# Residual sums as products on TensorE, turned tiles on four banks, and one weight item split by GpSimd in a two-block transformer

## The reference

```python
for i in range(DEPTH):                                     # first block
    h, gate = adaln_norm(x, c, norm_g[i], ada_w[i], ada_b[i])
    y = nsa_mixer(h, ...) if i % 2 == 0 else dilated_mixer(h, dil_w_in, dil_w_out)
    x = x + gate * y
x = rms_norm(x, final_g)
for layer in range(DEPTH):                                 # second block
    mix = _mixer_ab(x, ...) if layer % 2 == 0 else _mixer_cd(x, ...)
    x = _layer_norm(DEEPNORM_ALPHA * x + mix, ln1_g[layer], ln1_b[layer])
    ffn = (silu(x @ w_gate) * (x @ w_up)) @ w_down         # width 2816
    x = _layer_norm(DEEPNORM_ALPHA * x + ffn, ln2_g[layer], ln2_b[layer])
```

## Time and profile before

| what | value |
|---|---|
| median of 3 runs | 1098.12 us (1096.86 to 1101.09) |
| the profiled execution's own time | 1096.86 us |
| its span, first to last instruction | 1095.1 us |
| mean granted TensorE clock | 0.974 |
| busy TensorE, VectorE, ScalarE, GpSimd | 92%, 59%, 43%, 10% |

### The profile page before, as it was taken

How to read it: one execution, slowest core, us unless ns; L and a number is a source line. 1 busy time by engine, 2 the same in 40 slices (tenths; PEclk the granted TensorE clock), 3 DMA queues, 4 the chain that set the end, 5 groups by cost and what they waited for, 6 DMA issues and landing times.

```text
span 1095.1 us, 15848 instructions
## 1 busy us (share of the span) xinstructions
PE 1005.4 (92%) x6078; PEld 849.6 (78%) x6078; DVE 648.6 (59%) x1118; ACT 475.8 (43%) x740; POOL 114.3 (10%) x106
## 2 busy tenths in 40 slices
PE   5989989889998998898999999997998889999994
PEld 2889655668997778877778888876997768888884
DVE  4346354774662566535766666666454586666666
ACT  1243543624455623475334444433447534444440
POOL 3004101310970001100010000000001000000000
PEclk9999998999999899998999999999999999999997
DMA  9953254334452445321464554532532154555440
GB/s 378 354 203 131 88 221 154 119 152 150 157 210 83 187 148 185 120 77 40 166 219 172 184 206 184 178 145 93 213 141 78 70 187 166 180 206 189 172 172 39
DMA packets 23382, 178.41 MB, mean 163 GB/s; under 512 B 3711, under 2 KB 4143, under 8 KB 6823
## 3 DMA queue, kind: packets, MB, share of 16 engines
q1 hardware_dynamic: 19120, 166.70, 41.3%
q0 software_dynamic: 2224, 8.94, 2.4%
q10 hardware_dynamic: 1991, 2.14, 0.6%
HBM read 176.72 MB, written 1.05 MB: 162 GB/s over the span
## 4 chain that ended last, share of the span: by engine, by line
PE 75%; DVE 15%; ACT 4%; DMA 3%; issue 2%; ACTq 1%; POOL 0%; SPq 0%; DVEq 0%; POOLq 0%
PE G L858 12%; PE G L860 12%; PE G L859 12%; PE S L953 8%; PE T L953 7%; PE S L952 3%; PE T L952 3%; PE T L523 3%; PE T L442 2%; PE G L537 1%; PE G L539 1%; PE G L538 1%; DVE wlo L1624 1%; PE G L381 1%; DVE wlo L1621 1%
## 5 line engine op out<-in xcount | busy, mean ns | idle before, releaser
L858 PE MATMUL G<-whi,hTh 128*128 128x256 f32 (+4 forms) x688 | 222.5, 323 | 14.0 <-DVE hTl L459 5.5
L859 PE MATMUL G<-wlo,hTh 128*128 128x256 f32 (+4 forms) x672 | 211.1, 314 | 0.0
L1722 DVE TENSOR_TENSOR wlo<-ring,whi 128x2048 fp32r<-128x2048 f32 x88 | 154.4, 1758 | 90.3 <-ACT whi L1409 64.8
L860 PE MATMUL G<-whi,hTl 128*128 128x256 f32 (+4 forms) x624 | 192.3, 308 | 0.0
L858 PEld LDWEIGHTS G<-whi,hTh 128*128 128x128 f32 x688 | 132.4, 192 | 22.8 <-DVE hTl L459 7.1
L1621 DVE TENSOR_TENSOR wlo<-ring,whi 128x1024 fp32r<-128x1024 f32 (+2 forms) x60 | 92.7, 1586 | 68.5 <-ACT whi L1307 68.3
L859 PEld LDWEIGHTS G<-wlo,hTh 128*128 128x128 f32 x672 | 129.5, 193 | 3.7 <-issue 1.3
L953 PE MATMUL S<-hT,whi 128*128 128x512 f32 x352 | 129.3, 401 | 3.3 <-DVE hT L459 3.3
L953 PE MATMUL T<-hT,whi 128*128 128x512 f32 x352 | 126.5, 394 | 0.0
L860 PEld LDWEIGHTS G<-whi,hTl 128*128 128x128 f32 x624 | 120.5, 193 | 0.7
L1404 ACT CAST whi<-ring 128x2048 fp32r<-128x2048 f32 x44 | 83.9, 1906 | 17.9 <-PE S L1019 17.6
(11 more groups left out here) (305 smaller groups left out, 1823.8 us busy)
## 6 DMA issues: line engine op xcount, KB each, us to landing
ring<-in_ffn SPq DMA_DIRECT2D x44, 1536.0 KB, 6.3
ring<-in_ada_w SPq DMA_DIRECT2D x16, 1024.0 KB, 5.3
ring<-in_dil_w_in SPq DMA_DIRECT2D x16, 1024.0 KB, 4.8
ring<-in_cd_w_in SPq DMA_DIRECT2D x10, 1232.0 KB, 5.3
ring<-in_nsa_w_in SPq DMA_DIRECT2D x8, 1432.0 KB, 8.8
early<-in_ada_w SPq DMA_DIRECT2D x8, 1024.0 KB, 17.2
ring<-in_ab_w_in SPq DMA_DIRECT2D x4, 1440.0 KB, 6.2
vec<-in_vecs POOLq DMA_DIRECT2D x11, 512.0 KB, 5.0
```

The lines of the kernel that those rows point to most:

```text
L858: pe.matmul(out_, act_h, w_h, start=first_, stop=False)
L859: pe.matmul(out_, act_h, w_l, start=False, stop=False)
L860: return pe.matmul(out_, act_l, w_h, start=False, stop=last_)
L1722: TT(wlo[b][:, part], ring[:, b, part], whi[b][:, part].bitcast(F32), ALU.subtract).then_inc(st[what + "_lo"], 1)
```

## The change

- **Residual as a product.** In the second block's FFNs, TensorE multiplies ALPHA times the identity (`alpha_ident`, in `tok`) by `x` into the FFN's output banks ahead of its products (`residual`), which then accumulate on top. `ffn_out` reads the banks directly for statistics and for the subtraction.
- **Halves.** The last step of each LayerNorm is written in two halves of 512 columns, each with its own signal; turns and the store of the output go by halves.
- **Border order.** `dn`'s first low part comes after the turn's low parts; in `cd_in` both items of the first chunks are split before tile 1's norm, and the second chunk is whole before tile 1's turn; uq's low part comes after the latents' turns.
- **Entrances.** The `_rot` turns use four banks; ScalarE copies even groups and VectorE odd ones. Groups of later heads (four each in dil, ab and cd) are turned inside pairs 0 and 1, in G2 and G3, and copied by VectorE.
- **GpSimd.** It makes high and low parts of item 1 of `ab_out` and `cd_out`, once the entrance's turns are out.
- **Sinks.** No accumulation on ScalarE's exponentials; the sinks are exponentiated by themselves and added to the sums that the product with v already gives.
- **dil.** The gate is multiplied in per pair, the shares later, for tile 0 on VectorE and for tile 1 on ScalarE; the low parts of dil_out's items move (`low_quarters` makes item 0's in quarters, two at p = 8 and two behind the shares).

```diff
+        APART = ("ab_out", "cd_out")
...
+        alpha_ident = tok[:, 0, 0:P]
+        def bank_of(name, j, t):
+            return G[2 * t + j] if name == "cd_in" else G[2 * j + t]
...
+            if name in APART and m == 1:
+                return item_low, APART.index(name) + 1
...
+        SHARED = ("nsa_rot", "dil_rot", "ab_rot", "cd_rot")
...
+        SHARED_BANKS = TB + S
+        def wait_turned(eng, name):
+            groups, _, t0, _, _ = turns[name]
+            eng.wait_ge(turn["taken"], t0 + (len(groups) + 1) // 2)
+            eng.wait_ge(turn["drawn"], drawn0[name] + len(groups) // 2)
...
-                if g >= 2 and turn_bank(name, g) is turn_bank(name, g - 2):
+                if g >= 4 and name in SHARED:
+                    pe.wait_ge(*((turn["drawn"], drawn0[name] + g // 2 - 1) if g % 2 else (turn["taken"], t0 + g // 2 - 1)))
...
+                if name in SHARED and g % 2 == 1:
+                    continue
...
+        def turn_draw(dve, name):
+            groups, g0 = turns[name][0:2]
+            for g in range(1, len(groups), 2):
+                dve.wait_ge(turn["turned"], g0 + g + 1)
+                take = groups[g][1][0]
+                dve.tensor_copy(take[2], turn_src(name, g, take)).then_inc(turn["drawn"], 1)
+        def weave_turn(pe, name, k):
+            if k >= 2:
+                pe.wait_ge(woven["taken"], woven0[name] + k - 1)
+            for b, (src, width) in enumerate(woven_groups[name][k][0]):
+                ins = pe.transpose(G[3 - k % 2][0:width, b * P:(b + 1) * P], src, ident)
+            ins.then_inc(woven["turned"], 1)
+        def weave_draw(dve, name, k):
+            dve.wait_ge(woven["turned"], woven0[name] + k + 1)
+            rows, cols, dst, n = woven_groups[name][k][1][0]
+            dve.tensor_copy(dst, G[3 - k % 2][rows[0]:rows[1], cols[0]:cols[1]].rearrange("p (n c) -> p n c", n=n)).then_inc(woven["taken"], 1)
...
+                if sink is not None and 2 * p < n and sink(2 * p) is not None:
+                    rows = slice(2 * p, 2 * p + 2)
+                    dve.wait_ge(att["maxes"], 2 * (b0 + 2 * p + 2))
...
+                        dve.wait_ge(ab_s["sink_exp"], p - 5)
+                        summed = den[:, rows, :].unsqueeze(3)
+                        done(TT(summed, summed, o[:, :, :, DH:DH + 1], ALU.add))
...
-                            act_.activation(s[:, 0:1 + P], s[:, 0:1 + P], ACT.Exp, bias=negmax[:, h, 0:1], scale=-1.0,
-                                            accum_out=den[:, h, 0:1]).then_inc(att["probs"], 1)
...
+                        act_.activation(s[:, 1:1 + P], s[:, 1:1 + P], ACT.Exp, bias=negmax[:, h, 0:1], scale=-1.0).then_inc(att["probs"], 1)
+                        act_.activation(s[:, 1 + P:1 + SW], s[:, 1 + P:1 + SW], ACT.Exp, bias=negmax[:, h, 1:2],
+                                        scale=-1.0).then_inc(att["probs"], 1)
...
+                    if sink(2 * p - 2):
+                        rows = slice(2 * p - 2, 2 * p)
+                        act_.wait_ge(ab_s["sink_in"], p - 4)
+                        act_.activation(den[:, rows, :], den[:, rows, :], ACT.Exp).then_inc(ab_s["sink_exp"], 1)
...
-        dil_rot = rows_to(qT, blocks_of(tok)) + rows_to(kT, blocks_of(rotk))
+        dil_rot = [dil_q[0], dil_q[2], dil_k[0], dil_k[2]]
...
+        woven_groups = {"dil": [dil_q[1], dil_q[3], dil_k[1], dil_k[3]],
+                        "ab": rows_to(q2T, blocks_of(u[:, :, 672:1184])) + rows_to(q2T[:, 4:6, :], blocks_of(kswa)),
+                        "cd": rows_to(q2T, blocks_of(u[:, :, 1544:2056])) + rows_to(q2T[:, 4:8, :], blocks_of(u[:, :, 2056:2568]))}
...
-                sp.wait_ge(norm["ready"], norm_ready(8) - 1 + t)
-                sp.dma_start(out[:, t * P:(t + 1) * P, :].rearrange("b p d -> p (b d)"), x[:, t, :]).then_inc(stored, 16)
+                for half, (sig, value) in enumerate(((norm["half"], norm_half(8) + 1 + t), (norm["ready"], norm_ready(8) - 1 + t))):
+                    cols = slice(half * 512, (half + 1) * 512)
+                    sp.wait_ge(sig, value)
+                    sp.dma_start(out[:, t * P:(t + 1) * P, cols].rearrange("b p d -> p (b d)"), x[:, t, cols]).then_inc(stored, 16)
...
+            def split_item(name):
+                n = first[name] + 1
+                pool.wait_ge(landed[n % 2], 16 * (n // 2 + 1))
+                pool.wait_ge(used, split0[name] - 1)
+                raw, half = ring[:, n % 2, 0:OUT_K * OUT_W], OUT_K * OUT_W // 2
+                for part in range(2):
+                    cols = slice(part * half, (part + 1) * half)
+                    tl.done(pool.tensor_copy(out_high(1)[part], raw[:, cols]))
+                    ins = pool.tensor_tensor(out_low(1)[part], raw[:, cols], out_high(1)[part].bitcast(F32), ALU.subtract)
+                ins.then_inc(item_low, 1)
...
+            wait_turned(pool, "ab_rot")
+            split_item("ab_out")
...
-                chunk_part(1, 0, range(KT // 2))
+                turn_after = KT if name == "cd_in" else KT // 2
+                ins = chunk_part(1, 0, range(turn_after))
...
                 turn_pe(pe, turn_name, ready, 1)
-                chunk_part(1, 0, range(KT // 2, KT)).then_inc(st["full"], 1)
+                if turn_after < KT:
+                    chunk_part(1, 0, range(turn_after, KT)).then_inc(st["full"], 1)
                 if behind is None:
...
+            def residual(i, t, free):
+                pe.wait_ge(ffn[i]["alpha_set"], 1)
+                pe.wait_ge(outp["taken"], free)
+                for half in range(2):
+                    pe.matmul(G[2 * t + half][:], alpha_ident, x[:, t, half * 512:(half + 1) * 512], start=True, stop=False)
...
-                down(0, 0, True, False)
+                down(0, 0, False, False)
...
+                    if name in APART and n == 1:
+                        pe.wait_ge(item_low, APART.index(name) + 1)
...
+                        pe.wait_ge(*((norm["ready"], norm_ready(i) - 1 + g // 2) if g % 2 else (norm["half"], norm_half(i) + 1 + g // 2)))
...
+            def second_half(name, i, base):
+                def behind(p):
+                    if p < 2:
+                        weave_turn(pe, name, 2 * p)
+                        weave_turn(pe, name, 2 * p + 1)
+                    if p == 2:
+                        pe.wait_ge(woven["taken"], woven0[name] + 4)
+                    if p == 8:
+                        turn_half(i, 0, att["outs"], base + 4)
+                return behind
+            att_pe(pe, "ab", second_half("ab", 2, pairs0))
             project_out(2, "ab_out", None, (att["outs"], pairs0 + 8), "f0", norm_tiles(5))
-            keep_busy(5)
+            residual(0, 0, 11)
+            keep_busy(4)
             turn_pe(pe, "f0", norm_tiles(5), 1)
...
                 high(name, 0, 0, KT * w)
+                if name == "cd_in":
+                    high(name, 0, 1, KT * w)
                 turn_act(sc_e, turn_name, 0)
-                high(name, 0, 1, KT * w)
+                if name != "cd_in":
+                    high(name, 0, 1, KT * w)
...
+            sc_e.wait_ge(dil_s["share"], 1)
+            for g in range(3):
+                cols = slice(offs[g] * DH, offs[g + 1] * DH)
+                ins = sc_e.activation(tok[:, 1, cols], tok[:, 1, cols], ACT.Copy, scale=share[:, 1, g:g + 1])
+                if g > 0:
+                    ins.then_inc(shared_ready, 1)
...
-                    if p == 2:
-                        high_out(name, 1)
...
+            def scale_halves(i, b, t):
+                for half, sig in enumerate((norm["half"], norm["ready"])):
+                    cols = slice(half * 512, (half + 1) * 512)
+                    done(STT(x[:, t, cols], x[:, t, cols], rstd[:, t:t + 1], b[:, cols], ALU.mult, ALU.add), sig)
...
+            def set_gated(p, o, summed, r):
+                set_pair(p, o, summed, r)
+                cols = slice(2 * p * DH, (2 * p + 2) * DH)
+                done(TT(tok[:, :, cols], tok[:, :, cols], u[:, :, 3 * D + 2 * p * DH:3 * D + (2 * p + 2) * DH], ALU.mult))
...
+                if gatev is None:
+                    done(TS(alpha_ident, ident, ALPHA, None, ALU.mult), ffn[i - 2]["alpha_set"])
...
                 turn_low(dve, turn_name, 1)
+                low_ffn(st, 0, 0, dn, "dn")
                 low_ffn(st, 0, 1, gu, "gu")
...
+            def ffn_out(i, name, n, g, b, turn_name=None, lows=None):
...
+                    moments([G[2 * t + half][:] for half in range(2)], t, 2, True, EPS_LN)
                     for half in range(2):
-                        part = x[:, t, half * 512:(half + 1) * 512]
-                        done(STT(part, part, ALPHA, G[2 * t + half][:], ALU.mult, ALU.add))
-                        done(dve.bn_stats(bstat[:, t, half, :], part))
-                    finish(t)
+                        cols = slice(half * 512, (half + 1) * 512)
```

(45 more changed lines are left out.)

157 lines of the change are left out of this document (99 added, 58 removed).

## The result

The changed kernel took 1070.07 us as a median of four runs (1065.55 to 1073.16), beside 1099.2 for the kernel before (also four runs); the ratio is 0.9724, with a 95% interval of 0.9679 to 0.9770. The ratio times the 1098.12 of the table is 1067.8: 30 us gained, where 22 were forecast. The profiled execution took 1067.20 us against 1096.86, 29.7 less, with a sum of 22.3 to hold against it.

What follows compares the result with a forecast made beforehand. It took TensorE, with 75% of the chain (VectorE 15%), to bound the kernel, with gains only where it stands. Terms summed to 22.3 us: 1096.86 - 22.3 = 1074.6, plus 1.26, gave 1076, range 1069 to 1086.

Steps and rivals of the forecast that it cites:

- dil out: Before dil's last turns: gating moved into eight pairs, shares split over two engines, to gain 1.0 us [0 to 1.8].
- latents: Before ab: uq's low part, moved behind the latents' first low part, removes most of TensorE's 4.03 us wait: 2.4 gained.
- below 1069 only if nearly every high end holds: Whole kernel: a time under 1069 us needs almost all terms at their high ends; all high ones give 1068.
- ab's pairs: ab attention: without item 1's splits, seven pairs follow at 3.05 us each; with sinks' 0.4, 5.0 gained [2 to 6.5].
- the idle that preceded the 0.81 is gone: First FFN's first 9 us: 1.7 us of full clock is lacking, and half, 0.9, comes back.
- wanted only by the first down product: Borders into FFNs: dn's low part, 1.14 us of VectorE, can come behind the turn's low parts.
- Woven turns: Attentions: head groups turned inside the first pairs cost TensorE 2.2 us in dil and 1.65 in ab and cd.
- GpSimd's item: ab and cd: four GpSimd instructions for item 1 take 10.3 us clean or 32.6 contended, costing 0, up to 3 lost.
- Pairs bound by TensorE at 3.4: Rival, chance 0.15: attention pairs stay at 3.4 us, the sum falls to 14.4, the time is 1084 us.
- Residual products exposed: Rival, chance 0.07: at FFN borders, 7.1 us of products less two fillers gives 5.3 back; 1081 us.
- GpSimd late: Rival, chance 0.05: TensorE waits for item 1 in both projections, 3 us in each; 1082 us.
- Slower: Rival, chance 0.02: GpSimd takes 47 us for four instructions, ending at 528 and 880; 1104 us.

Runs made afterwards that it cites:

- e1: The kernel before, run again without an edit for a second trace: 1104.39 us.
- e9: The changed kernel with cd_in's start in the old order (second item's low part behind tile 1's norm, half the second chunk behind the turn, old banks): 1068.50 us, single execution.
- e8: The changed kernel with the residual of both FFNs added by VectorE again and one full-width subtraction: 1077.91 us, single execution.
- e3: The changed kernel with dn's first low part back ahead of the turn's low parts: 1072.15 us.
- e7: The changed kernel with uq's low part ahead of the latents' low parts again: 1073.88 us, single execution.
- e4: The changed kernel with GpSimd's three bias loads put off until four low parts of dn are done in the first FFN: 1069.64 us.
- e6: The changed kernel with all turns of the four entrances on two banks, drawn by ScalarE, none woven into pairs: 1074.02 us, single execution.
- e11: The changed kernel run again without an edit for a third trace: 1074.27 us, ratio 0.9813 to the kernel before.
- e12: The kernel before, run again without an edit for a third trace: 1090.47 us.
- e2: The changed kernel, run again without an edit for a second trace: median 1074.06 us, ratio 0.9833 to the kernel before.

## Why the forecast was right in its parts and 8 us short in the first comparison

Stages of the changed kernel against those of before, each from the trace with the least clock lost in it:

| term of the sum | forecast | before | changed | gain |
|---|---|---|---|---|
| start and nsa entrance | 0.4 | 117.61 | 117.26 | 0.35 |
| dil entrance and pairs | 1.4 | 35.67 | 33.59 | 2.1 |
| dil out, to x0's turn | 1.0 | 35.19 | 32.54 | 2.7 |
| x0's turn to ab's turn (latents) | 2.4 | 61.08 | 57.15 | 3.9 |
| ab entrance and pairs | 5.0 | 38.28 | 31.36 | 6.9 |
| ab_out | 0 | 30.23 | 30.39 | -0.2 |
| border ahead of the first FFN | 0.65 | 8.59 | 7.65 | 0.94 |
| first FFN | 0.9 | 184.55 | 187.35 | -2.8 |
| first FFN's end to tile 1's turn | 4.9 | 19.80 | 14.92 | 4.9 |
| cd entrance and pairs | 1.4 | 34.54 | 31.71 | 2.8 |
| border ahead of the second FFN | 0.65 | 8.58 | 7.65 | 0.93 |
| second FFN | 0.9 | 183.16 | 183.14 | 0 |
| end | 2.7 | 13.83 | 11.31 | 2.5 |
| sum | 22.3 | | | 25.1 |

The sum of the last column agrees with all executions together: 25 of the kernel before have their median at 1097.99, 14 of the changed one at 1073.05, 24.9 apart. This backs the sum and not each row, since the rows take the traces with the least clock lost, and an execution loses more. By the means of three traces each, the changed kernel is 29.4 faster: 4.0 of that is the nsa stage, which has no row, cd's row is 4.5 (e1's falls), ab's is 5.6, and ab_out is 1.3 slower and not 0.2. The new wait of 1.9 at ab's entrance, for VectorE's draws, has a fall behind it in two of the changed kernel's three traces.

**The step that failed: "below 1069 only if nearly every high end holds".** 1067.8 came, with more than half of the high ends not reached. Between the two profiled executions 29.7 us were gained, 7.4 more than the sum. Of these 29.7, 8.4 lie ahead of the end of dil_in: 4.0 in the start, where the sum had 0.4, and 4.4 from there through the nsa attention, its projection and dil_in, where it had nothing (219.34 against 214.95, with 6.8 and 3.4 of clock lost). The change has next to nothing in that stretch, and the kernel before took 222.90 and 214.41 there in its other traces. I had made the range from bounds of costs alone and put the difference between executions of one kernel at nothing. The three comparisons gave ratios of 0.9724, 0.9833 and 0.9813; on 1098.12 the last two are 1079.8 and 1077.6, in the range. Behind dil_in the pair of traces gained 21.3 where the sum had 21.9. That this comes so close is luck: several terms were too low, by up to 2.3 (dil out), one was too high by 4.6 (the first FFN), and one of -1.8 (ab_out) I did not have.

**Right, with its size.** cd_in's start (4.9 forecast, 4.9 measured, e9), the end (2.7 and 2.5, e8), both borders (0.65 and 0.94), the dil entrance itself (2.79, forecast 2.9), ab's entrance (1.8, forecast 1.7) with the wait for VectorE's draws where I put it, and ab's pairs at 2.9 to 3.0, forecast 3.05, but for the first of 2.70 and one of 3.38. The end's 2.5 is two errors that nearly cancel: VectorE saved 0.94 a tile and not 1.4, and the last store gave 0.6 where I took next to nothing. GpSimd ran in attention at no more than its clean price (2.37 for 1024 columns, where two rows of 512 give 2.58). With that the trace agrees with the Trainium skill (GPSIMD Engine Reference, 1. Specifications), by which GpSimd contends with VectorE's instructions in a two-port mode or with two SBUF inputs; VectorE's maxima beside it read PSUM and one table.

**A step of the sum that failed: "the idle that preceded the 0.81 is gone: 9 us at 0.81 lack 1.7 us of full clock; I take half, 0.9".** I charged the clock at two borders only. At the first FFN it does come back once the new wait is away (184.55 to 183.05 in e3, 1.5 for my 0.9); the second FFN has no fall in the first two traces of before and could return nothing. Clock is lost behind other waits which this change also shortens. Behind the latents' wait it is 1.7 to 3.1 in the three traces of before and 0 in the changed kernel's; e7 puts the wait back and gets 4.7 for my 2.4. That term came out 1.5 over, and the clock is the reason. Dil out lost 5.1 in all three traces of before and 0, 5.1 and 0 in the changed kernel's. In ab's pairs the clock (3.4 in all three of before, none at the casts' place in the changed kernel's) also came back, but my step from the measured turns to a pace of 3.05 already held it without naming it; ab's 1.9 over is some 0.75 of hidden woven turns, and the rest a pace just under 3.05 and the sinks' 0.4, which did not show. The earlier trace rows showed the 0.62 there, and I used it for a rival instead of asking where else waits are followed by it.

**A second one: dn's low part, "wanted only by the first down product".** It was wanted by the ring as well. I followed item_low through the ring of two slots and not this one. Its new place lets the slot go 9.5 us later against the FFN's start, into three bias loads, and the FFN is 2.8 slower at least where I had 0.9 gained (e3, e4).

**Mis-sized.** Woven turns: about half of their work is hidden (e6), so dil, ab and cd give some 0.8, 0.75 and 0.65 more than forecast from that. Cd's are 16 transposes, 2.2 of work, and I charged ab's 1.65. GpSimd's item: 6.8 us, below my clean bound of 10.3. dil out: 2.7 between e1, which loses 5.1 of clock there, and e11, which loses none; 0.3 between e12 and e2, which both lose 5.1; no run undid this part by itself, so how much is clock stays open.

**The rivals.** Pairs bound by TensorE at 3.4: out (2.9 to 3.0). Residual products exposed: 0.37 a border, not 2.65. GpSimd late: it ended at 471.6, item 1's first product stands at 503.4. Slower: nothing of it showed.

What stays open is why the same program's clock falls in one execution and not in another at the same place, as in the nsa stage (214.41 to 222.90 in three traces of before, 213.27 to 220.81 in those of the new order), and why e9's wait of 3.1 brought no fall.

## What to carry to other kernels

A low part or cast that "nobody needs yet" may still hold a buffer: before moving it, follow the slot it frees to the next load, and count what else is on the queues then. Where waits shrink, the clock behind them can come back as well, nearly as much again in the latents and behind the casts of this kernel, but not in e9; so look in the trace for the stretch at half level behind a wait, and price it as a possible gain of its own. A range needs the spread of one kernel's executions beside the bounds of the costs. When executions of one kernel differ by more than the effect, compare stage by stage between named instructions, at equal clock: this told 0.4 us apart where the runs' times could not tell 5.

## What the runs showed of the hardware

- One program, one core: the kernel before ran from 1086.89 to 1108.69 us over 25 executions, and its traces granted 0.959 to 0.974 of the clock on the mean. Every fall was to the lower level (PEclk 0.50 in the middle of the stretch), for 3 to 14 us.
- A GpSimd cast of 128x1024 took 1.04 us, as ScalarE's does; its subtraction of the same size 2.37, against VectorE's 1.22.
- Statistics that read PSUM took 1.43 for two, as from SBUF (0.69 each in e8).
- A 1.5 MB load took 12.2 us beside three loads of 512 KB on GpSimd's queue (read over shifted rows), and 6.5 and 6.6 without them (e3, e4); the median of all of its kind is 6.4 in the first trace.
